# Spreading two rows of roots by transfers, and moving the group roots into the sixth step of the second attention

## The reference, cut to what matters

```python
def rmsnorm(x, g):
    xf = x.astype(jnp.float32)
    y = xf * lax.rsqrt(jnp.mean(xf * xf, axis=-1, keepdims=True) + EPS)
    return (y * g.astype(jnp.float32)).astype(x.dtype)
...
# first layer: h = rms_norm(x, norm_g); proj = h @ w_in; forgetting attention, pooling,
#              stick-breaking attention; x = x + mixed @ w_out
# second layer:
h = rmsnorm(x, mix_pre_norm)
z = h @ w_in
a = mla(...)                    # latent attention: 8 heads, queries and keys of 64 + 32 numbers
c = short_gated_conv(...)       # c_gate * xv, three taps, times b_gate
m = jnp.concatenate([rmsnorm(a, attn_group_norm), rmsnorm(c, conv_group_norm)], axis=-1)
x = x + rmsnorm(m @ w_out, mix_post_norm)
# then a gated feed-forward layer of width 2816, and a gate by a position-wise embedding
```

## Time and profile before

| what | us |
|---|---|
| median of 3 runs | 897.89 |
| the profiled execution | 898.09 |
| its span | 896.4 |
| TensorE busy in it | 889.4 |
| GpSimd busy | 500.5 |
| VectorE busy | 403.0 |
| ScalarE busy | 342.9 |

### The profile page before, as it was taken

The page is one execution under the profiler, slowest core; times in us unless marked ns, Lnnn a source line. Parts: engine busy times, 40 slices in busy tenths (PEclk is TensorE's granted clock), DMA queues, the critical chain, the costliest instruction groups (busy, mean ns, idle before and its releaser), DMA issues.

```text
span 896.4 us, 12958 instructions
## 1 busy us (share of the span) xinstructions
PE 889.4 (99%) x4520; PEld 734.5 (82%) x4520; DVE 403.0 (45%) x699; ACT 342.9 (38%) x693; POOL 500.5 (56%) x523
## 2 busy tenths in 40 slices
PE   9999999999999999999999999999999999999998
PEld 7889887777779888887779888888888888888887
DVE  2763485678642643876667511111111112223672
ACT  4333403567725130566648532222222223233421
POOL 6988785331475877843336564444444445555453
PEclk9999999999999999999999999999999999999999
DMA  6342362212222322221213332233322322223213
GB/s 219 96 139 81 109 167 100 66 60 82 72 81 71 132 95 90 79 87 48 69 51 99 113 117 94 94 102 103 100 94 94 118 94 94 95 99 108 71 51 118
DMA packets 29725, 86.25 MB, mean 96 GB/s; under 512 B 5224, under 2 KB 8192, under 8 KB 29680
## 3 DMA queue, kind: packets, MB, share of 16 engines
q1 hardware_dynamic: 24528, 78.65, 26.3%
q10 hardware_dynamic: 5152, 6.99, 2.9%
HBM read 80.93 MB, written 2.10 MB: 93 GB/s over the span
## 4 chain that ended last, share of the span: by engine, by line
PE 97%; DVE 1%; POOL 1%; ACT 0%; issue 0%; POOLq 0%; ACTq 0%; DVEq 0%
PE bank L545 28%; PE bank L547 28%; PE bank L546 28%; PE bank L602 5%; PE bank L790 2%; PE bank L893 1%; POOL w_lo L472 1%; PE bank L1135 1%; PE bank L1136 1%; PE bank L885 1%; PE bank L1134 1%; PE bank L922 1%; PE bank L857 0%; PE bank L769 0%; PE bank L854 0%
## 5 line engine op out<-in xcount | busy, mean ns | idle before, releaser
L472 POOL TENSOR_TENSOR w_lo<-raw,w_hi 128x256 fp32r<-128x256 f32 (+1 forms) x420 | 409.0, 1002 | 205.6 <-ACT w_hi L1386 199.8
L545 PE MATMUL bank<-aT_hi,w_hi 128*128 128x512 f32 (+1 forms) x584 | 225.8, 387 | 0.0
L547 PE MATMUL bank<-aT_hi,w_lo 128*128 128x512 f32 (+1 forms) x584 | 222.4, 381 | 0.0
L546 PE MATMUL bank<-aT_lo,w_hi 128*128 128x512 f32 (+1 forms) x584 | 222.2, 380 | 0.0
L545 PE MATMUL bank<-w_hi,aT_hi 128*128 128x512 f32 (+3 forms) x576 | 218.5, 379 | 0.8 <-POOL w_lo L472 0.4
L547 PE MATMUL bank<-w_hi,aT_lo 128*128 128x512 f32 (+3 forms) x576 | 213.1, 370 | 0.0
L546 PE MATMUL bank<-w_lo,aT_hi 128*128 128x512 f32 (+3 forms) x576 | 212.9, 370 | 0.0
L464 POOL TENSOR_SCALAR w_hi<-raw 128x1024 fp32r<-128x1024 f32 x70 | 76.0, 1086 | 168.1 <-PE bank L547 135.6
L1386 ACT ACTIVATE w_hi<-raw 128x1024 fp32r<-128x1024 f32 x70 | 74.1, 1060 | 231.1 <-PE bank L547 214.9
L547 PEld LDWEIGHTS bank<-aT_hi,w_lo 128*128 128x128 f32 x584 | 109.8, 188 | 21.2
L545 PEld LDWEIGHTS bank<-aT_hi,w_hi 128*128 128x128 f32 x584 | 110.0, 188 | 19.9 <-issue 0.2
(11 more groups left out here) (247 smaller groups left out, 916.3 us busy)
## 6 DMA issues: line engine op xcount, KB each, us to landing
raw<-in_weights SPq DMA_DIRECT2D x141, 512.0 KB, 3.3
x<-in_x ACTq DMA_DIRECT2D x4, 512.0 KB, 5.3
y_out<-x SPq DMA_DIRECT2D x7, 256.0 KB, 4.1
x<-in_x SPq DMA_DIRECT2D x3, 512.0 KB, 8.5
g_post<-in_gains ACTq DMA_DIRECT2D x3, 512.0 KB, 3.4
k_twice<-k_twice ACTq DMA_DIRECT2D x2, 512.0 KB, 5.5
x<-in_x SPq DMA_DIRECT2D x2, 256.0 KB, 3.5
raw<-in_weights SPq DMA_DIRECT2D x2, 256.0 KB, 4.6
```

The lines of the kernel that those rows point to most:

```text
L472: lo = nc.gpsimd.tensor_tensor(w_lo[:, s, at], raw[:, r, at], w_hi[:, s, at].bitcast(F32), ALU.subtract)
L545: mm(out, st_hi, mv_hi, start=start, stop=False)
L546: mm(out, st_hi, mv_lo, start=False, stop=False)
L547: return mm(out, st_lo, mv_hi, start=False, stop=stop)
```

## The change: what it does

The turns that make `R1` and `R2`, their two tiles and VectorE's two copies go. Instead ScalarE issues a transfer of the roots from their columns to a row in memory (`roots_to_row`) as soon as it knows them, and later one that reads this row to all 128 partitions of `R` (`row_to_all`). VectorE waits for the latter (`R_in`) where it copied, or a little later. In the second attention the group roots are taken in step 5 on VectorE, `out2c`'s first tile leaves its bank in ScalarE's step 6 and not 4, and low part 7 is made in step 7, not 3.

```diff
@@ -95,7 +95,6 @@
     group("fk", (0, 1, 2, 3), "act", ("fk", 3))
-    tiles["R1", 0] = (7, "dve", None)
     group("sf", (4, 5, 6, 7), "act", ("sf", 2))
...
     group("lkv", (5, 6, 7, 2), "act", ("lkv", 1))
-    tiles["R2", 0] = (3, "dve", None)
...
         R = sb("R", [P, S])
+        r_rows = nc.dram_tensor("r_rows", (2, S), F32).ap()
...
@@ -725,11 +725,6 @@
             weights_moving([("fk", t) for t in range(T)], group4("fk"), S)
-            pe.wait_ge(r_made, 1)
-            bank_free(("R1", 0))
-            for t in range(T):
-                last = turn(tbank(("R1", 0))[:, t * P:(t + 1) * P], stat[:, 3, t:t + 1].broadcast_to([P, P]))
-            last.then_inc(tile_full, 1)
...
@@ -1023,11 +1018,6 @@
-            pe.wait_ge(r_made, 2)
-            bank_free(("R2", 0))
-            for t in range(T):
-                last = turn(tbank(("R2", 0))[:, t * P:(t + 1) * P], stat[:, 2, 4 + t:5 + t].broadcast_to([P, P]))
-            last.then_inc(tile_full, 1)
             def turn_lats():
...
@@ -1461,8 +1451,19 @@
+            def roots_to_row(n, of):
+
+                act_.dma_start(r_rows[n, :].rearrange("(t p) -> p t", p=P), of, allow_slow_non_contiguous=True)\
+                    .then_inc(r_row_out, 16)
+
+            def row_to_all(n):
+
+                act_.wait_ge(r_row_out, n * 16 + 16)
+                act_.dma_start(R[:, :], r_rows[n:n + 1, :].broadcast_to([P, S])).then_inc(R_in, 16)
+
             act_.wait_ge(const_in, 48)
             act_.wait_ge(r_made, 1)
+            roots_to_row(0, stat[:, 3, 0:T])
             qk_rows("fq", 0)
...
             heads_hi("qT", q_parts, col("gq"), q_hi)
+            row_to_all(0)
             qk_rows("fk", T)
...
             act_.wait_ge(r_made, 2)
+            roots_to_row(1, stat[:, 2, 4:4 + T])
...
             rsqrt(slice(48, 56))
+            row_to_all(1)
...
-                if m % 4 == 0 and 0 < m <= 32:
+                if m == 6 or m % 4 == 0 and 4 < m <= 32:
                     g, t = (m // 4 - 1) // T, (m // 4 - 1) % T
-                    if m == 4:
+                    if m == 6:
                         act_.wait_ge(group_rsqrt, 1)
...
@@ -2019,10 +2023,8 @@
-            full(dve, ("R1", 0))
-            drain(("R1", 0), V.tensor_copy(R[:, :], tbank(("R1", 0))[:, :]))
-            dve.wait_ge(drained["dve"], order[0])
             qk_norm(T)
+            dve.wait_ge(R_in, 16)
...
-            full(dve, ("R2", 0))
-            drain(("R2", 0), V.tensor_copy(R[:, :], tbank(("R2", 0))[:, :]))
-            dve.wait_ge(drained["dve"], order[0])
+            dve.wait_ge(R_in, 32)
             own(V.memset(u[:, :, 0:KERNEL - 1], 0.0))
...
             def q2_late(m):
-                if m < 4:
-                    q2_low_part(4 + m)
-
-            roots(slice(60, 64))
-            V.tensor_tensor(stat[:, 3, 60:64], stat[:, 3, 60:64], stat[:, 3, 4:8], ALU.mult).then_inc(group_rsqrt, 1)
+                if m in (0, 1, 2, 7):
+                    q2_low_part({0: 4, 1: 5, 2: 6, 7: 7}[m])
+                elif m == 5:
+                    roots(slice(60, 64))
+                    V.tensor_tensor(stat[:, 3, 60:64], stat[:, 3, 60:64], stat[:, 3, 4:8], ALU.mult)\
+                        .then_inc(group_rsqrt, 1)
+
             for i in range(4):
                 q2_low_part(i)
```

More of the change, by code:

```diff
@@ L323, in hybrid_kernel @@
         masks_made, ident_made = sem("masks_made"), sem("ident_made")
-        w_half, r_made, R_made = sem("w_half"), sem("r_made"), sem("R_made")
+        w_half, r_made = sem("w_half"), sem("r_made")
+        r_row_out, R_in = sem("r_row_out"), sem("R_in")
         gate_scaled, gate_made = sem("gate_scaled"), sem("gate_made")
```

## The result

| kernel | us, median (lowest to highest) | executions |
|---|---|---|
| before, same chip | 897.96 (897.45 to 898.82) | 22 |
| changed | 901.29 (898.83 to 1104.12) | 22 |

The ratio is 1.0035, with an interval of 1.0028 to 1.0043: the change makes the kernel 3.3 us slower, where I had forecast 1.8 us faster. (The 1104.12 is a single execution at a mean granted clock of 0.753, which the ratio leaves out; the others lie between 898.83 and 903.63.) The profiled execution of the changed kernel took 901.2 us with a span of 899.5, against 898.09 and 896.4 before, so the trace holds the loss: 3.1 us.

What follows compares the result with a forecast made beforehand. TensorE was taken as the bound, busy 889.4 of 896.4 us. Turns 0.86 plus second attention 0.95 gave 1.81 us, taking the 897.89 median to 896.1; forecast's own range 895.9 to 896.4, whole range 895.6 to 897.1.

Steps and rivals of the forecast that it cites:

- The nearest transfer of single numbers: Price of writing 512 roots to memory: no longer than the 2.7 us of a load of 1024 numbers.
- the last rival: Root write issued at 27.8 us holds weight loads beyond GpSimd's lead; price 3.6 us, time 899.7; chance 0.05.
- the estimated lead of 1.8: Thinnest place from 26 to 60 us: low parts end at 40.45, TensorE takes the chunk at about 42.2.
- The argument "against it": Against transfers getting in the way: a load of 1024 numbers at 33 us runs there and TensorE does not wait.
- The turns: Both places where TensorE turned a row of roots: removing the turns gains 0.43 us each, 0.86 together.
- The start of the second attention: VectorE's chain starts sooner without the group roots ahead of the first low part: gain 0.95 us.
- the 7.83 us stay: Second attention: VectorE's stretch from first low part to maximum 3 keeps its length, so maximum 3 starts 0.95 us sooner.
- The 0.71 goes whole: Second attention: the 0.71 us lost between the products beside steps 3 and 4 vanishes entirely.
- The roots in step 5: Second attention: four root operations on VectorE take about 0.8 us beside an idle GpSimd and cost TensorE zero.
- the rival with long roots: Roots in step 5 take 2.53 us, TensorE loses 0.8, gain 1.0 us, time 896.9; chance 0.08.
- that of the worthless head start: Second attention: something unseen sets maximum 3, only the turns' 0.86 us counts, time 897.0; chance 0.09.
- The whole healing: Second attention: the last 0.34 us of wait goes too, gain 2.15 us, time 895.7; chance 0.10.

Runs made afterwards that it cites:

- spare_wide: `late_write` plus an unread write of 512 single roots at 27.7 us, each into its own 64-byte line: 896.55 us, ratio 0.9987.
- spare_half: `late_write` plus an unread write of 256 single roots, side by side in memory, at 27.7 us: 899.4 us, ratio 1.0028.
- att_only: Kernel before with only the second attention's edits, both rows of roots still by TensorE's turns: 897.58 us, ratio 0.9989.
- the exchanged copy: `late_write`, with ScalarE in step 3 of the second attention copying step 0's turned weights ahead of its exponential: 896.23 us, ratio 0.9981.
- late_write: Changed kernel with the first write of roots issued near 60 us, not 27.7, and read back near 77 us: 896.57 us, ratio 0.9980.
- sbuf_row: Changed kernel with roots written into partition 0 of R by four transfers of 128, then to memory as one 2 KB run: 896.55 us, ratio 0.9981.
- twice: Changed kernel with the first write of 512 single roots made twice, the second into a spare row: 902.24 us, ratio 1.0049.
- rows_only: Changed kernel without the second attention's edits, only both rows of roots by transfers: 904.0 us, ratio 1.0052.

## Why the prediction was wrong, step by step

**The step that failed** is the size of one term: "The nearest transfer of single numbers in the trace has 1024 of them and lands in 2.7 us; half as many should not take longer." It took 11.1. The row I took it from is a load: it reads single numbers from memory. The new transfer writes them into memory, and the kernel before has no such write. `spare_wide` and `spare_half` show that what counts is not even the direction alone but where single numbers are put (2.3 us apart, 8.7 for half as many side by side). I bounded the price from both sides by rows of another kind, so the bound was none.

The Trainium skill (DMA: Bandwidth & Descriptors, Specifications) says that below 512 bytes the transfer engine reads, modifies and writes. I weighed the sentence and dismissed it by the 2.7 us. It pointed the right way for the changed kernel (10.9 to 11.1 us), but its bound does not sort these runs: pieces of 16 bytes (2.9 us) and single numbers 64 bytes apart (2.3 us) are also below 512 and were fast.

**The second half of the step: others are held too.** I asked only when the write would be needed (94.4 us), not whom it holds while it runs. I had this as the last rival, with 0.05. Its mechanism is what happened, and its lead was right. Before, the chunk's low parts ended at 40.45; in the changed kernel they end at 45.20:

```profile
41.30 1.05 POOL L464 TENSOR_SCALAR w_hi<-raw 128x1024 fp32r<-128x1024 f32 x1 [7.79 <-DMA raw<-in_weights]
42.43 2.77 POOL L472 TENSOR_TENSOR w_lo<-raw,w_hi 128x256 fp32r<-128x256 f32 x4
```

That is 4.75 us late; less the estimated lead of 1.8 it leaves 2.95, and TensorE waited 3.02. (GpSimd's own hole is longer, 7.79 us; it starts 6.9 later and wins 2.15 back, since these low parts take 2.77 us and not 4.92.) The rival's stall was even too long: 5.4 less 1.8 is 3.6, where the trace has 3.30 with its start. Its 899.7 is 1.6 below what was measured because it had no other price: the half clock added 1.65, and the attention brought 0.26 less than its 0.95.

**The argument "against it" was empty.** That the load of gains runs in this stretch and TensorE does not wait says that a load is harmless, and nothing of a write. With it the chance of 0.05 was too low; a transfer whose kind no row shows, issued where the lead is 1.8 us, deserved several times that.

**The turns: right.** Forecast 0.86; the shifts give 0.44 + 0.43 = 0.87. Reads back to all partitions took 3.1 to 4.2 us over all runs, inside the bound of 2.7 to 5.4, and were hidden as said.

**The start of the second attention: right in kind, 0.95 forecast, 0.68 measured** from the scores of step 0 to the turn of step 5 (8.52 us before, 7.84 after; 0.69 by the shifts, 0.63 us of median in `att_only`). VectorE's timeline after, which answers to the earlier trace rows:

```profile
387.87 0.69 DVE L2332 TENSOR_TENSOR aT_hi<-bank,q_high 96x512 fp32r<-96x512 f32 x1 [2.27 <-ACT q_high L1376]
...
392.76 0.73 DVE L2104 TENSOR_SCALAR h<-h,erec 128x128 f32<-128x128 f32 x1
...
395.99 0.69 DVE L2097 TENSOR_REDUCE negmax<-bank 128x1 f32<-128x512 f32 x1
...
398.85 0.16 DVE L1929 TENSOR_TENSOR stat<-stat 128x4 f32<-128x4 f32 x1
399.05 0.36 DVE L1902 SCALAR_TENSOR_TENSOR stat<-stat 128x4 f32<-128x4 f32 x2
...
399.65 0.56 DVE L2097 TENSOR_REDUCE negmax<-bank 128x1 f32<-128x384 f32 x1
```

And TensorE's, which answers to the earlier trace rows:

```profile
394.50 0.48 PE L545 MATMUL bank<-w_hi,aT_hi 128*128 128x512 f32 x1
...
396.05 0.47 PE L545 MATMUL bank<-w_hi,aT_hi 128*128 128x512 f32 x1
...
397.81 0.52 PE L602 MATMUL bank<-ident,h 128*128 128x128 f32 x3 [0.40 <-ACT PT L1376]
398.08 0.48 PE L545 MATMUL bank<-w_hi,aT_hi 128*128 128x512 f32 x1
```

The first low part starts 0.04 behind the first high part (387.25 + 0.58), as said. Against the scores of step 0 (386.07 before, 389.97 after) low part 0 starts 0.97 us sooner, as forecast, and maximum 3 only 0.68. So "the 7.83 us stay" is what did not hold: from low part 0 to maximum 3 it is 8.12, because the scaling of step 0 took 0.73 us instead of 0.44. GpSimd was splitting beside it in both kernels. What differs is how early in one of GpSimd's subtractions the scaling begins. Before:

```profile
389.44 0.74 POOL L472 TENSOR_TENSOR w_lo<-raw,w_hi 128x256 fp32r<-128x256 f32 x1
389.83 0.44 DVE L2102 TENSOR_SCALAR h<-h,erec 128x128 f32<-128x128 f32 x1
```

After:

```profile
392.67 0.73 POOL L472 TENSOR_TENSOR w_lo<-raw,w_hi 128x256 fp32r<-128x256 f32 x1
392.76 0.73 DVE L2104 TENSOR_SCALAR h<-h,erec 128x128 f32<-128x128 f32 x1
```

Each time the scaling ends some 0.08 us behind the subtraction (390.27 and 390.18; 393.49 and 393.40), and in all thirteen traces it does so to 0.01 us, 0.44 to 0.79 long; the same form takes 0.29 where GpSimd is idle (398.65 in the changed kernel). So it is held until that subtraction ends, and being sooner moved it to a worse moment.

"The 0.71 goes whole" did not hold either: the step from the product beside 3 to that beside 4 is 1.55 and not 1.29, since TensorE got there 0.23 sooner (from the scores of step 0 to the product beside it took 0.41 for 0.60) and low part 6 was 0.29 late. This moved waiting from one step to the other and took nothing more. The wait in step 5 is left at 0.57 where I had 0.34. The gain is the 0.23 and the 0.45 of the step from 3 to 4 (2.00 less 1.55), together 0.68.

**The roots in step 5: right.** From 398.85 to the next maximum at 399.65 is 0.80 us, the row of the idle GpSimd, and nobody waits in step 8. So the rival with long roots is out, and so is that of the worthless head start (0.68, not 0). The whole healing did not come by itself: it took the exchanged copy. `late_write` has all the gains of my sum and no write in the way: 1.64 us below before, against a forecast of 1.81.

**Still open.** The traces show that the loads' packets stand for 2.2 us each while single numbers side by side are written, but not what they stand for, nor why two rows at once cost no more than one; the runs bound it by place and layout only. Whether the 64 bytes of `spare_wide` are more than is needed, and whether its spread over 32 KB or the line for each number is what helps, was not tried.

## What to carry to other kernels

Before a new transfer is booked as hidden, ask of it what is asked of any instruction: who else uses the thing it occupies, and how much lead they have at that moment. Price a transfer by a row with the same direction and the same layout at its destination, and if there is none, say that its price is unknown and give the rival that lives on it a chance to match. Single numbers that must become a row go side by side into the core's own memory, as in `sbuf_row`, or to memory where the loads have a longer lead, as in `late_write`; runs of 16 bytes are as short, if the reader can take their order, which no run here did. A stall of 3 us on TensorE is booked with the matmuls behind it at the granted clock, not by its length alone.

## What the runs showed of the hardware that was not expected

- A write of 512 numbers of 4 bytes side by side in memory takes 9.2 to 11.1 us; 256 of them 8.7; 512 in lines of 64 bytes 2.3; 128 runs of 16 bytes side by side 2.9; four transfers of 128 into one partition of the core's memory 2.2 each. Two of the slow ones, issued together, take 11.0 and 10.9.
- While such a write runs, loads of 512 KB on another engine's queue take 8.4 us (median of three, one of them 10.9) in place of 3.2 to 3.3. The Trainium skill says of transfers between cores (DMA: Bandwidth & Descriptors, Back-pressure in remote DMA) that stalled writes stall the other queues of their transfer engine; what is seen here, on one core and into memory, looks like it (0.92 of the transfer engines' time at 61 GB/s, 2.2 us for a packet of a load), but no view shows which engine or queue stalls.
- After a stall of 3.0 us the granted clock was 0.72 from 46 to 52 us and cost 1.65 us; it was 0.72 too in `twice` after 3.5 and 0.50 in `rows_only` after 3.6. After the 2.2 us of `spare_half` it stayed 1.00 in the trace, but not in four of its ten executions.
- A VectorE scaling of 128x128 numbers that starts beside a GpSimd subtraction ends 0.08 to 0.09 us behind it in all thirteen traces: 0.44 to 0.79 us long for 0.29.
